# Two sample blocks through one pass of the output and query projections, with the second block's router scores kept and searched later

## The chip, the cores and the metric

The kernel runs on one core of one Trainium2 chip. The metric is the device time of one execution in microseconds (us). All arithmetic is float32. The profile was taken in one execution of its own. That execution has no separate total beside its span, so spans are compared with spans, and the distance from span to timed median is taken as it stands.

## The reference, cut to what matters

A two-layer network works on one block of 128 prompt tokens and on 256 sample tokens, which are two blocks of 128. Per layer and stream:

```
h = layer_norm(x) * (1 + sc1) + sh1
mix = concat(diff_attention, mla, gqa)(h @ w_in) @ w_out        # 20 score maps; a sample block reads 384 keys, the prompt 128
x = layer_norm(alpha * x + g1 * mix, ln1_g, ln1_b)
h = layer_norm(x) * (1 + sc2) + sh2
q = h @ peer_wq ; s = q . keys                                   # 8 retrieval heads, 2 x 128 scores each
top-16 of each half, top-16 of their 256 sums -> 128 experts and gates per token
act = gelu(h . u[expert]) ; ff = sum(gate * act * v[expert])     # u, v: rows of 1024 floats, gathered per token
x = layer_norm(alpha * x + g2 * ff, ln2_g, ln2_b)
```

The experts differ from token to token, so each token block gathers 128 rows of `u` and 128 rows of `v` per token in each layer.

## The kernel before, in words

Five engines each run their own in-order program, made from one list of steps, `STEPS`, written by `plan()`. A step is (kind, layer, stream, block, index). Block 0 is the prompt, blocks 1 and 2 are the sample blocks.

The gathers are the backbone. A step `u` or `v` stands for gathers of 128 rows of 4 KB (0.52 MB each), issued by GpSimd (POOL, L596) into a ring of 15 tiles, `expert`. A `u` tile is consumed by VectorE (DVE, L1434: a dot product for each token), a `v` tile by TensorE (PE, L895: an accumulation into the PSUM tile `acc`, four tiles at a time). Gather number g may be issued only when tile g - 15 has been consumed. Each of the six pairs (layer, block) has 256 gathers: 40 `u` first, then groups of four `v` and four `u`, then the last `v`. I number these six stretches weave 1 to weave 6: prompt, block 1 and block 2 of layer 0, then the same of layer 1.

`weave(l, b, side)` lays other work between the gathers of a pair. Each side step has a planned cost in the table `COST`, and gathers follow in proportion to the cost that has gone by. So the more side work a weave has, the more of it stands between two groups of gathers. The side work of weave k is what weave k + 1 needs, since the indices of a block's experts must be known before its gathers. The side steps that matter here:

- `fin` (DVE, L1466 to L1475): closes the weave before, reads `acc`.
- `ln1`, `h_t`, `win`, `prep`, `k_t`, `cache_t`, `kv_mla`: first norm, transposes, input projection and keys of a stream.
- `q_t`, `q_rope`, `qm_t`, 23 `heads` steps, `mix`: the attention of one block. A full `heads` step has a score matmul (L787), three transposes (L794) and three value matmuls (L814) of three different maps on PE, a maximum on DVE, an exponential and a copy on ScalarE (ACT).
- `wout`: four tiles of the output projection (L706). `ln_x`, `ln_h`: the norms behind it.
- `route`: nine steps, eight with a tile of the query projection (L838) and the matmuls of the scores (L848) one step later.
- `topk` (L1363 to L1382) and `pick` (L1392 to L1421): the search for the 16 best of a retrieval head, and the experts' numbers, all on DVE.
- `idx_t`: transposes the numbers for the `v` gathers. `row`: spreads a row of `mods` over the partitions.

Weights come in tiles of 0.4 to 1.2 MB through a ring of three, `wt`, issued by SyncE (SP, L543) in the order of use. Gathers and weight tiles use the same 16 DMA engines. Before the change `block_steps(l, s, b)` runs attention, `wout`, norms, `route`, `topk` and `pick` for one block, so `w_out` and `peer_wq` with the keys are loaded for each of the three blocks. Scores go to `rs`, two heads deep, and are searched at once.

## Time and profile before

| | us |
|---|---|
| median of 3 timed runs | 2509.18 (2507.83 to 2509.75) |
| span of the profiled execution | 2504.9 |
| outside the span: median less span | 4.3 |
| first gather issued, last gather issued | 215.8, 2475.9 |
| DVE busy, PE busy, POOL busy | 1636.7, 1719.9, 1492.5 |

The page cuts the span into 40 slices of 62.6 us. "DMA" is the mean busy share of the 16 DMA engines. The windows used below run from the first gather of a weave to the first gather of the next, so one window is one weave.

### The profile page before, as it was taken

Reading aid. Unit: us, or ns where it says so; the run is one execution under the profiler, and the core shown is the slowest. Engines: PE = TensorE matmul, PEld = TensorE weight load, DVE = VectorE, ACT = ScalarE, POOL = GpSimd, SP = SyncE. Lnnn points to the kernel's source line nnn. Section 1 sums busy time; section 2 is a strip of 40 time slices with the busy share of each in tenths; the row PEclk is TensorE's granted clock in tenths of the full one; section 3 lists DMA queues with packets and bytes.
Section 4 is the critical chain, followed back from the end, with each engine's and each line's share of the span. In section 5 each row is a group of like instructions: output and inputs, shape, how many; then the busy total and the mean of one; then the engine's idle time right before and its main releaser. Section 6 shows DMA issues by size and latency. Waiting matters only on the chain.

```text
span 2504.9 us, 24629 instructions
## 1 busy us (share of the span) xinstructions
PE 1719.9 (69%) x8433; PEld 838.7 (33%) x8433; DVE 1636.7 (65%) x4033; ACT 334.8 (13%) x990; POOL 1492.5 (60%) x1583
## 2 busy tenths in 40 slices
PE   5888469778287767277877368897738777545557
PEld 3566334442143422132344044355214342101101
DVE  2338886677975782854668857568886568774451
ACT  0410003211131100101111110331112110000000
POOL 1104467656676665666665656665677666777773
PEclk9988789989698878678899678798859889878889
DMA  9768999999999999999999989999999999999996
GB/s 389 305 254 341 412 353 407 411 413 409 410 409 412 406 412 412 374 413 410 410 413 413 378 333 410 411 358 411 411 409 409 412 411 410 409 403 409 410 410 271
DMA packets 248333, 980.67 MB, mean 391 GB/s; under 512 B 28001, under 2 KB 29681, under 8 KB 232849
## 3 DMA queue, kind: packets, MB, share of 16 engines
q0 software_dynamic: 226944, 847.35, 85.1%
q1 hardware_dynamic: 19536, 130.80, 13.0%
q8 instruction: 67, 1.10, 0.2%
q10 hardware_dynamic: 1728, 0.95, 0.1%
q14 instruction: 58, 0.47, 0.0%
HBM read 976.47 MB, written 2.52 MB: 391 GB/s over the span
## 4 chain that ended last, share of the span: by engine, by line
DMA 42%; PE 23%; DVE 19%; POOL 9%; issue 5%; ACT 2%; DVEq 0%; ACTq 0%; POOLq 0%
DMA expert<-in_experts,eidx_t 31%; DVE expert L1434 10%; PE acc L895 10%; POOL expert L596 9%; DMA expert<-in_experts,eidx 8%; PE mmb L696 3%; PE mmb L838 3%; PE mmb L706 2%; DMA expert<-in_w_mod 2%; PE mmb L787 1%; DMA wt<-in_w_wq 1%; ACT hT L975 1%; PE acc L651 1%; PE ob L814 1%; DVE small L1140 1%
## 5 line engine op out<-in xcount | busy, mean ns | idle before, releaser
L1434 DVE CUSTOM_DVE_ANT_0 expert<-expert,hb 128x1024 f32<-128x1024 f32 x768 | 910.0, 1218 | 355.1 <-DMA expert<-in_experts,eidx 335.3
L895 PE MATMUL acc<-expert,strip 128*32 128x512 f32 x3072 | 829.2, 708 | 328.2 <-DMA expert<-in_experts,eidx_t 325.9
L596 POOL DMA_INDIRECT expert<-in_experts,eidx x768 | 734.7, 957 | 491.5 <-PE acc L895 206.8
L596 POOL DMA_INDIRECT expert<-in_experts,eidx_t x768 | 733.2, 955 | 311.4 <-issue 205.7
L895 PEld LDWEIGHTS acc<-expert,strip 128*32 128x32 f32 x3072 | 148.9, 119 | 906.7 <-DMA expert<-in_experts,eidx_t 724.6
L838 PE MATMUL mmb<-hT,wt 128*128 128x128 f32 x1536 | 195.9, 290 | 27.7 <-DMA wt<-in_w_wq 22.8
L838 PEld LDWEIGHTS mmb<-hT,wt 128*128 128x128 f32 x1536 | 189.0, 205 | 51.5 <-issue 45.5
L696 PE MATMUL mmb<-wt,hT 128*128 128x244 f32 x768 | 172.6, 385 | 7.3 <-ACT hT L975 4.8
L696 PEld LDWEIGHTS mmb<-wt,hT 128*128 128x128 f32 x768 | 150.7, 199 | 35.4 <-issue 14.4
L869 PE MATMUL trb<-ident,acts 128*128 128x128 f32 x24 | 9.6, 398 | 194.9 <-DVE acts L1454 194.9
L567 POOL DMA_DIRECT2D expert<-in_w_mod x40 | 21.3, 536 | 181.0 <-PE acc L651 181.0
L1303 DVE TENSOR_REDUCE neg_max<-mmb 128x1 f32<-128x384 f32 (+1 forms) x120 | 54.9, 465 | 101.7 <-PE mmb L787 101.0
L787 PE MATMUL mmb<-area 32*128 32x384 f32 (+5 forms) x240 | 93.0, 494 | 10.1 <-ACT area L1049 5.9
L686 PE MATMUL trb<-ident,tok 128*128 128x128 f32 x144 | 29.3, 338 | 102.1 <-DVEq L1259 61.4
L706 PE MATMUL mmb<-wt,hT 128*128 128x256 f32 x384 | 92.0, 397 | 3.9 <-ACT hT L982 2.7
L912 ACT ACTIVATE area<-mmb 128x256 f32<-128x256 f32 (+3 forms) x126 | 48.5, 387 | 327.8 <-PE mmb L838 290.1
L706 PEld LDWEIGHTS mmb<-wt,hT 128*128 128x128 f32 x384 | 74.5, 198 | 28.2 <-issue 10.0
L1049 ACT ACTIVATE area<-mmb,neg_max 128x384 f32<-128x384 f32 (+1 forms) x120 | 60.8, 507 | 108.9 <-DVE neg_max L1303 108.5
L869 PEld LDWEIGHTS trb<-ident,acts 128*128 128x128 f32 x24 | 3.9, 163 | 207.9 <-DVE acts L1454 201.9
L676 PE MATMUL mmb<-mods,sel 128*128 128x512 f32 x144 | 70.7, 618 | 0.3 <-ACT rows L912 0.3
L1363 DVE MAX8 area<-area 128x8 f32<-128x128 f32 x96 | 23.3, 284 | 69.9 <-ACT area L912 69.3
L1099 ACT ACTIVATE gelu<-gelu 128x32 f32<-128x32 f32 x24 | 5.5, 229 | 472.4 <-DVE gelu L1446 472.4
(177 smaller groups left out, 1615.8 us busy)
## 6 DMA issues: line engine op xcount, KB each, us to landing
wt<-in_w_wq SPq DMA_DIRECT2D x48, 1152.0 KB, 8.4
expert<-in_w_mod POOLq DMA_DIRECT2D x40, 1024.0 KB, 9.3
wt<-in_w_win SPq DMA_DIRECT2D x32, 976.0 KB, 8.1
wt<-in_w_wout SPq DMA_DIRECT2D x24, 1024.0 KB, 8.1
expert<-in_experts,eidx POOLq DMA_INDIRECT x768, 14.0
expert<-in_experts,eidx_t POOLq DMA_INDIRECT x768, 14.0
wt<-in_w_mod SPq DMA_DIRECT2D x8, 1024.0 KB, 8.4
wt<-in_w_uq SPq DMA_DIRECT2D x6, 384.0 KB, 7.0
```

What stands on the lines that cost most here:

```text
L596: pool.indirect_dma_start(expert[:, g % RING, :], None, table, bass.IndirectOffsetOnAxis(at, 0)).then_inc(landed[g % RING], 16)
L676: pe.matmul(mm_bank(mm + half)[:], sel[:, e:e + 1].to_broadcast([P, P]), mods[:, half * 512:half * 512 + 512], start=True, stop=True).then ...
L686: m = pe.transpose(bank[:, q * P:(q + 1) * P], src[:, c * P:(c + 1) * P], ident[:])
L696: m = pe.matmul(bank[:, jj * 256:jj * 256 + IN_C], hT[:, kt, B[jj] * P:(B[jj] + 1) * P], w[:, kt * IN_C:(kt + 1) * IN_C], start=kt == 0, s ...
L706: m = pe.matmul(bank[:, 0:256], hT[:, kt, b * P:(b + 1) * P], w[:, kt * 256:(kt + 1) * 256], start=kt == 0, stop=kt == KT - 1)
L787: pe.matmul(bank[:, 0:K], q_, k_, start=True, stop=True).then_inc(sc_full, 1)
L838: m = pe.matmul(bank[:, i * P:(i + 1) * P], w[:, kt * 256 + i * P:kt * 256 + (i + 1) * P], hT[:, kt, b * P:(b + 1) * P], start=kt == 0, st ...
L895: m = pe.matmul(acc[32 * i:32 * i + 32, cs], strip[:, q % 2, i, at:at + 32], expert[:, (g + i) % RING, cs], start=k < 4, stop=False, skip_ ...
L912: act.activation(dst, src_of(mmb[u % 2]), ACT.Copy).then_inc(mm_free, 1)
L1049: act.activation(E[:, m % 2, 0:K], mmb[at_mm[m] % 2][:, 0:K], ACT.Exp, bias=neg_max[:, m:m + 1], accum_out=row_sum[:, m:m + 1]).then_inc(m ...
L1303: v.tensor_reduce(neg_max[:, m:m + 1], mmb[at_mm[m] % 2][:, 0:K], X, ALU.max, negate=True).then_inc(nmax_ready, 1)
L1434: v.tensor_tensor_reduce(expert[:, r, :], expert[:, r, :], hb[:], 1.0, 0.0, ALU.mult, ALU.add, dots[:, k:k + 1]).then_inc(dot_ready, 1)
```

## The change

Both sample blocks' attention is done first. Then one pass over the four `wout` tiles and the eight `wq` tiles serves both: `wout` multiplies each tile with both blocks one after the other, `route` streams 256 token columns past each weight. Block 1's scores go to `rs` and are searched at once, as before. Block 2's go to `kept`, which lies where the keys were, and are searched in the next weave by `search_steps`. Block 2's activations live in `tok2`, in `wide`. The prompt's layer-1 work up to its attention moves from weave 3 to weave 2, and a wait on `idx_ready` keeps its keys from overwriting `kept`. The gain rows `row` are spread once for both blocks.

```diff
+JOINT = {"wout": 7.2, "route": 2.4}
 def cost_of(x):
-    c = COST[x[0]]
+    c = JOINT.get(x[0], COST[x[0]]) if x[2] == "S" else COST[x[0]]
...
+def block_steps(l, s):
+    b = BLOCKS[s][0]
+    out = [x for c in BLOCKS[s] for x in head_steps(l, s, c)]
     out += [("wout", l, s, b, n) for n in range(OUT_T)]
-    out += [("ln_x", l, s, b, i) for i in range(3)] + [("ln_h", l, s, b, 0), ("h_t", l, s, b, 2)]
+    out += [("ln_x", l, s, c, i) for i in range(3) for c in BLOCKS[s]]
+    for c in BLOCKS[s]:
+        out += [("ln_h", l, s, c, 0), ("h_t", l, s, c, 2)]
...
+def search_steps(l):
+    half = R_HEADS // 2
+    return [x for e in range(2) for x in
+            [("topk", l, "S", 2, half * e + i) for i in range(half)]
+            + [("pick", l, "S", 2, 2 * e + i) for i in range(2)] + [("idx_t", l, "S", 2, e)]]
...
-    steps += weave(0, 0, search + [x for x in sample if x[0] != "win"] + key_steps(0, "S") + block_steps(0, "S", 1), project)
-    steps += weave(0, 1, fins(0, 0) + block_steps(0, "S", 2) + mod_steps(1, (4, 5)) + [("cols", 1, "", 0, 1)])
-    steps += weave(0, 2, fins(0, 1) + ln1_steps(1, "P", 0) + win_steps(1, "P") + key_steps(1, "P") + block_steps(1, "P", 0))
+    again = ln1_steps(1, "P", 0) + win_steps(1, "P") + key_steps(1, "P") + block_steps(1, "P")
+    mix = again.index(("mix", 1, "P", 0, 0))
+    steps += weave(0, 0, search + [x for x in sample if x[0] != "win"] + key_steps(0, "S") + block_steps(0, "S"), project)
+    steps += weave(0, 1, fins(0, 0) + search_steps(0) + mod_steps(1, (4, 5)) + [("cols", 1, "", 0, 1)] + again[:mix])
+    steps += weave(0, 2, fins(0, 1) + again[mix:])
     steps += weave(1, 0, fins(0, 2) + ln1_steps(1, "S", 1) + ln1_steps(1, "S", 2) + win_steps(1, "S") + key_steps(1, "S")
-                   + block_steps(1, "S", 1))
-    steps += weave(1, 1, fins(1, 0) + block_steps(1, "S", 2))
+                   + block_steps(1, "S"))
+    steps += weave(1, 1, fins(1, 0) + search_steps(1))
...
-                    for kt in range(KT):
-                        m = pe.matmul(bank[:, 0:256], hT[:, kt, b * P:(b + 1) * P], w[:, kt * 256:(kt + 1) * 256],
-                                      start=kt == 0, stop=kt == KT - 1)
+                    for jj in range(NB):
+                        for kt in range(KT):
+                            m = pe.matmul(bank[:, jj * 256:jj * 256 + 256], hT[:, kt, B[jj] * P:(B[jj] + 1) * P],
+                                          w[:, kt * 256:(kt + 1) * 256], start=kt == 0, stop=kt == KT - 1)
...
-                                m = pe.matmul(bank[:, i * P:(i + 1) * P], w[:, kt * 256 + i * P:kt * 256 + (i + 1) * P],
-                                              hT[:, kt, b * P:(b + 1) * P], start=kt == 0, stop=kt == KT - 1)
+                                m = pe.matmul(bank[:, i * NB * P:(i + 1) * NB * P],
+                                              w[:, kt * 256 + i * P:kt * 256 + (i + 1) * P],
+                                              hT[:, kt, b * P:(b + NB) * P], start=kt == 0, stop=kt == KT - 1)
...
                 if kind == "k_t":
+                    if s == "P" and l > 0:
+                        act.wait_ge(idx_ready, 2 * 3 * l)
...
+                        if s == "S":
+                            act.wait_ge(mm_full, n("mm_full", 0) + 1)
+                            act.activation(kept[:, e - 1], mmb[at_s % 2][:, 256:512].rearrange("p (i c) -> p i c", i=2),
+                                           ACT.Copy)
...
-                    halves = [(i, 2 * e + i, rs[:, e % 2, i, :]) for i in range(2)]
+                    halves = [(i, 2 * e + i, kept[:, e, i, :] if b == 2 else rs[:, e % 2, i, :]) for i in range(2)]
```

SyncE's loads from the last `win` tiles of layer 0's sample stream to the `mod` tiles, before:

```order
L543 DMA wt<-in_w_uq 128x768
L543 DMA wt<-in_w_wout 128x2048 x4
L543 DMA wt<-in_w_wq 128x2304 x8
L543 DMA wt<-in_w_uq 128x768
L543 DMA wt<-in_w_wout 128x2048 x3
L551 DMA cache<-in_cache 128x928
L543 DMA wt<-in_w_wout 128x2048
L543 DMA wt<-in_w_wq 128x2304 x8
L543 DMA wt<-in_w_mod 128x2048 x8
```

and of the change:

```order
L572 DMA wt<-in_w_uq 128x768 x2
L572 DMA wt<-in_w_wout 128x2048 x3
L580 DMA cache<-in_cache 128x928
L572 DMA wt<-in_w_wout 128x2048
L572 DMA wt<-in_w_wq 128x2304 x8
L572 DMA wt<-in_w_mod 128x2048 x8
```

One set of four `wout` and eight `wq` tiles is gone from each layer.

VectorE in the first `u` tiles of weave 2, from the end of `fin` on, before (L1434 is one `u` tile; 12 of them follow in a row, then the rope of block 2's attention):

```order
L1475 TENSOR_TENSOR x<-tmp,rows 128x1024
L1434 ISA expert,dots<-expert,hb 128x1024
L1434 ISA dots 128x1
L1434 ISA expert,dots<-expert,hb 128x1024
L1434 ISA dots 128x1
```

and of the change, where four `u` tiles (the last is the first row here) are followed by a whole `topk` (L1408 to L1428), and then by eight more `u` tiles and the next `topk`:

```order
L1480 ISA expert,dots<-expert,hb 128x1024
L1480 ISA dots 128x1
L1408 MAX area<-area 128x8 x2
L1411 MAX_INDEX i<-area 128x8
L1412 MATCH_REPLACE area<-area 128x128
L1411 MAX_INDEX i<-area 128x8
L1412 MATCH_REPLACE area<-area 128x128
L1417 MAX area<-area 128x8 x2
L1420 MAX_INDEX i<-area 128x8 x2
L1422 TENSOR_TENSOR area<-area 128x256
L1424 MAX area<-area 128x8
L1425 MAX_INDEX bi<-area 128x8
```

The search that stood behind block 2's own projections at the end of weave 2 now stands at its start, eight `topk` and two pairs of `pick` within the first 64 `u`.

TensorE between two groups of four `v` tiles (L895) in the attention of weave 4, before, four `heads` steps:

```order
L895 MATMUL acc<-expert,strip 32x512 x8
L787 MATMUL mmb<-area 128x384
L794 MATMUL trb<-ident,area 128x128 x3
L814 MATMUL ob<-wide,area 128x64 x2
L814 MATMUL ob<-cache,area 128x64
L787 MATMUL mmb<-area 128x384
L794 MATMUL trb<-ident,area 128x128 x3
L814 MATMUL ob<-area 128x64 x3
```

and of the change, the same stretch from its second step on (six steps stand between the two L927):

```order
L817 MATMUL mmb<-area 128x384
L824 MATMUL trb<-ident,area 128x128 x3
L844 MATMUL ob<-area 128x64 x3
L817 MATMUL mmb<-area 128x384
L824 MATMUL trb<-ident,area 128x128 x3
L844 MATMUL ob<-area 128x64 x3
L817 MATMUL mmb<-area 128x384
L824 MATMUL trb<-ident,area 128x128 x3
L844 MATMUL ob<-wide,area 128x64 x2
L844 MATMUL ob<-cache,area 128x64
L927 MATMUL acc<-expert,strip 32x512 x8
```

Where four or five `heads` steps stood between two groups of `v`, there are now six in weave 4 and five or six in weave 1.

## Rows read from the trace of the kernel before

**Rows 1.** The page, busy share of the DMA engines in 40 slices

```profile
DMA  9768999999999999999999989999999999999996
```

**Rows 2.** Windows, one a weave: us, busy time (count) by engine, PEclk, DMA share, GB/s

```profile
215.80:604.80 389.00, 283.60 (x1475) 168.07 (x1475) 296.68 (x777) 60.01 (x177) 244.51 (x256) 0.87 1.00 398
604.80:980.30 375.50, 262.51 (x1234) 113.17 (x1235) 265.95 (x639) 50.69 (x142) 245.58 (x257) 0.83 1.02 410
980.30:1379.80 399.50, 274.43 (x1258) 129.05 (x1252) 255.51 (x645) 48.79 (x161) 243.55 (x256) 0.82 1.01 406
1379.80:1781.80 402.00, 291.40 (x1460) 164.23 (x1459) 285.18 (x707) 67.50 (x189) 247.00 (x256) 0.82 0.97 385
1781.80:2146.60 364.80, 250.91 (x1158) 112.52 (x1158) 268.50 (x645) 49.24 (x137) 245.72 (x257) 0.84 1.03 410
2146.60:2475.90 329.30, 177.60 (x531) 33.69 (x532) 170.58 (x306) 10.09 (x33) 240.50 (x255) 0.81 1.02 408
```

**Rows 3.** Line L596, the gathers: who waited for them, and issue to landing

```profile
  DVE expert L1434: 335.3, 106
...
DMA to landing us min/median/max: 4.4/14.0/27.1
```

**Rows 4.** DMA issues of the two projections: count, KB each, us to landing

```profile
wt<-in_w_wq SPq DMA_DIRECT2D x48, 1152.0 KB, 8.4
wt<-in_w_wout SPq DMA_DIRECT2D x24, 1024.0 KB, 8.1
```

**Rows 5.** Timeline of DVE, weave 1: one topk, then u tiles

```profile
229.75 0.48 DVE L1363 MAX8 area<-area 128x8 f32<-128x128 f32 x2
...
235.42 1.22 DVE L1434 CUSTOM_DVE_ANT_0 expert<-expert,hb 128x1024 f32<-128x1024 f32 x1
...
236.57 1.22 DVE L1434 CUSTOM_DVE_ANT_0 expert<-expert,hb 128x1024 f32<-128x1024 f32 x1
```

**Rows 6.** Timeline of DVE: a pair of pick to the next topk; fin's middle piece

```profile
564.41 0.22 DVE L1392 CAST area<-i 128x128 f32<-128x128 uint32 x1
...
575.20 0.49 DVE L1363 MAX8 area<-area 128x8 f32<-128x128 f32 x2
...
630.01 1.22 DVE L1470 SCALAR_TENSOR_TENSOR tmp<-x,tmp 128x1024 f32<-128x1024 f32 x1
...
636.13 1.22 DVE L1434 CUSTOM_DVE_ANT_0 expert<-expert,hb 128x1024 f32<-128x1024 f32 x1
```

**Rows 7.** Windows of lost DMA time, same columns as rows 2

```profile
1040.00:1060.00 20.00, 8.21 (x24) 6.16 (x24) 19.29 (x43) 3.38 (x9) 11.73 (x13) 0.59 0.82 299
1420.00:1476.00 56.00, 15.59 (x66) 11.03 (x67) 45.45 (x99) 7.69 (x22) 25.29 (x27) 0.56 0.79 295
1640.00:1664.00 24.00, 20.65 (x115) 12.00 (x114) 16.34 (x37) 7.68 (x24) 11.65 (x13) 0.79 0.76 283
226.00:292.00 66.00, 26.95 (x138) 24.35 (x138) 60.49 (x170) 4.04 (x12) 39.12 (x42) 0.74 1.02 411
```

**Rows 8.** Timeline of PE, weave 4: heads steps at full and half clock

```profile
1631.18 0.91 PE L787 MATMUL mmb<-area 64*128 64x384 f32 x2
...
1633.11 0.91 PE L787 MATMUL mmb<-area 64*128 64x384 f32 x2
...
1606.62 1.64 PE L787 MATMUL mmb<-area 32*128 32x384 f32 x2 [0.52 <-ACT area L1049]
...
1610.20 1.64 PE L787 MATMUL mmb<-area 32*128 32x384 f32 x2
```

**Rows 9.** Timeline of PE, weave 4: route with scores and v; wout

```profile
1769.20 3.84 PE L838 MATMUL mmb<-hT,wt 128*128 128x128 f32 x32
1772.87 0.61 PE L848 MATMUL mmb<-wt,area 128*128 128x128 f32 x4
1773.41 1.92 PE L895 MATMUL acc<-expert,strip 128*32 128x512 f32 x16
...
1674.74 3.72 PE L706 MATMUL mmb<-wt,hT 128*128 128x256 f32 x16
```

More of the change, by code:

```diff
@@ L255, in rows_wanted @@
     kind, l, s, b, e = x
+    if kind == "ln_x" and b == 2:
+        return ()
     st = {"P": 0, "S": 1}.get(s, int(b > 0))
@@ L267, in after, with last_use @@
             return i - 2 if e == 0 else steps.index((kind, l, s, b, 0))
-        return steps.index({0: ("wout", l, s, b, OUT_T - 2), 2: ("ln_x", l, s, b, 0)}[e])
+        return steps.index({0: ("wout", l, s, b, OUT_T - 2), 2: ("ln_x", l, s, BLOCKS[s][-1], 0)}[e])
+    def last_use(i, x):
+        kind, l, s, b, e = x
+        return steps.index((kind, l, s, BLOCKS[s][-1], e)) if kind == "ln_x" else i
     put, released = {}, []
@@ L442, in trunk_program @@
                                                   (512,))
-        qT, rs, rep, cand, cand2, eq, v16, i16f, best, bf, e1 = views(
-            KV, AREA, (2, 2, P), (2, 2, P), (2, P), (16, 16), (256,), (4, TOPK, 16), (16, TOPK), (R_HEADS, 2, TOPK),
+        kept, qT = views(0, KV, (R_HEADS, 2, P), (2, 2, 2 * P))
+        rs, rep, cand, cand2, eq, v16, i16f, best, bf, e1 = views(
+            KV, AREA, (2, 2, P), (2, P), (16, 16), (256,), (4, TOPK, 16), (16, TOPK), (R_HEADS, 2, TOPK),
             (R_HEADS, TOPK), (SLOTS,), (SLOTS,))
@@ L548, in _ @@
                     if n > 0:
-                        end = max(i for i, y in enumerate(STEPS) if y[0] == "wout" and y[1] == n - 1 and y[3] == 2 and y[4] == 0)
+                        end = max(i for i, y in enumerate(STEPS) if y[0] == "wout" and y[1] == n - 1 and y[2] == "S" and y[4] == 0)
                         sp.wait_ge(mm_free, mm_after[end])
@@ L680, in _ @@
                     pe.wait_ge(tok_ready, n("tok"))
-                    src = tok[:]
+                    src = tok2 if (b, e) == (2, 2) else tok[:]
                     for half in range(2):
@@ L846, in scored @@
                         pe.wait_ge(mm_free, use + 1)
-                        for i in range(2):
-                            m = pe.matmul(bank[:, i * P:(i + 1) * P], qT[:, (e - 1) % 2, i, :],
+                        for jj, i in itertools.product(range(NB), range(2)):
+                            m = pe.matmul(bank[:, (2 * jj + i) * P:(2 * jj + i + 1) * P],
+                                          qT[:, (e - 1) % 2, i, jj * P:(jj + 1) * P],
                                           w[:, 2048 + i * P:2048 + (i + 1) * P], start=True, stop=True)
@@ L1344, in _ @@
                     if e == 2:
[L1345 to L1347 removed]
+                        link(v.tensor_tensor(y, y, row() if b < 2 else row_now[-2], ALU.mult))
+                        link(v.tensor_tensor(x[:, b, :], y, row() if b < 2 else row_now[-1], ALU.add))
+                        if b != 1:
+                            v.sem_inc(rows_used, 2)
                 if kind == "ln_h":
[L1350 removed]
+                    normed(tok2 if b == 2 else tok[:], x[:, b, :])
                     v.sem_inc(tok_ready, 1)
```

36 lines of the change are left out of this document (20 added, 16 removed).

## The prediction

> **What bounds the kernel now.** I read the page first. From the fifth slice to the last but one the DMA engines are busy at 9 tenths or more, with one slice at 8 [rows 1], so the transfers are the suspect and not an engine. The second view is one window for each weave [rows 2]. Weave 6 has no weight tile at all and takes 329.3 us for 256 gathers, 1.286 us each, at 408 GB/s. Weave 5 differs in its transfers only by one `uq`, four `wout` and eight `wq` tiles. By the sizes in [rows 4] these are 4 x 1.05 + 8 x 1.18 MB and 0.39 MB, 14.0 MB together, or 34 us at 410 GB/s. It takes 35.5 us longer. So a byte of weights costs its full time there. The third view is the line of the gathers: VectorE waits 335 us for them, and a gather lands 14.0 us after its issue where the least is 4.4 us [rows 3]. The difference, 9.6 us, is queueing. I take it as the cover of the ring: an engine may be 9.6 us late with its tiles before the DMA engines run dry. The fourth view is the stretches in which they did run dry [rows 7]. Against the full share of 1.02, they lose 4 us of 20 at 1040, 13 us of 56 at 1420 and 6 us of 24 at 1640. In the first two VectorE is the busy one (19.3 of 20 us at 1040), in the third TensorE (20.7 of 24). Time that the DMA engines lose is not made up, since POOL needs 240 to 247 us of its own for 256 gathers plus its issue gaps, and the transfers leave no room.
>
> **Weights no longer loaded.** SyncE's order shows four `wout` and eight `wq` tiles fewer in each layer: 8 x 1024 KB + 16 x 1152 KB = 27.3 MB. At 410 GB/s this is 66.5 us less transfer. Weaves 3 and 5 lose these loads, and part of the prompt's loads move from weave 3 to weave 2. This is the gain, if the DMA engines stay fed.
>
> **The kept search at the start of weave 2.** Before, `topk` stood beside `route` steps, whose tiles kept the DMA engines in work. Now eight `topk` and four `pick` stand with no load beside them, among the first 64 `u`. VectorE's work from `fin` to the last `pick`: 60 `u` at 1.15 us (start to start, [rows 5]) is 69.0; eight `topk` at 5.67 (229.75 to 235.42, [rows 5]) is 45.4; two pairs of `pick` at 10.8 (564.41 to 575.20, [rows 6]) is 21.6; `fin` is 6.1 (630.01 to 636.13) and three operations at 1.22 for the rest [rows 6], 9.8. Sum 145.8 us. In the same stretch 60 `u` and 28 `v` are gathered, 88 x 1.286 = 113.2 us. VectorE falls 32.6 us behind, the ring covers 9.6, and 23 us of transfer time are lost. Bounds: if the ring covers all 14.0 us of [rows 3] and the prefetched `mod` tiles fall into the gap (three of 1 MB, 7.7 us), 11 us; if nothing is covered, 33. The window from 226 to 292 speaks for the low end, for there VectorE was busy for 60.5 of 66 us and the DMA engines stayed at 1.02 [rows 7]; but `win` tiles stood beside that search. Weave 5's search, spread over a weave with nothing else in it, brings VectorE 2.9 us for each group of eight gathers beside 4.6 of `u`, against 10.3 of transfer: free.
>
> **TensorE in weaves 1 and 4.** Matmul work is moved, not saved. Prices: a full `heads` step 1.9 us at the 2.4 GHz level (granted clock 1.00; 1631.18 to 1633.11, [rows 8]); four `v` 1.9; a route tile 3.7 us for 32 passes of 128 columns; scores 0.54; a `wout` tile 3.7 us for 16 passes of 256 columns [rows 9]. A pass thus costs 0.115 us at 128 columns and 0.23 at 256: double. So I price a joint route step at 32 x 0.23 + 1.1 = 8.5 us and a joint `wout` at 7.4, each twice the old.
>
> In weave 4, the ten groups of eight gathers with attention and `wout` hold 40 full `heads` steps' worth, 76 us; transposes and latent queries of both blocks, some 8 (my estimate, from 16 transposes and the `uq` matmuls at the prices above); ten times four `v`, 19; `wout` 30; a gain row 2: 135 us. Transfers there: 103 + 4 x 2.56 + 1 = 114. Excess 21, less the cover: 11 us. In its routes, 36 gathers and eight tiles take 46.3 + 8 x 2.88 = 69 us, TensorE 68 + 8 x 1.9 + 4 = 87: excess 18, less the cover: 8 us, of which part was already lost before in the third stretch of [rows 7]. Before, 6 us were lost here, and I count 13 more. In weave 1, attention is spread thinner: 13 groups, 140 us of TensorE against 145 of transfer, nothing lost; its routes have 86 to 88 against 80, within the cover. At 1.2 GHz a `heads` step takes 3.6 us (1606.62 to 1610.20, [rows 8]). TensorE idles before the attention begins, as before, so I allow one more group of four to six steps at that level, 7 us. Term: +20. Bounds: 0 if the excess hides in a full cover of 14 us twice and the pieces overlap; 45 with no cover and two such groups.
>
> The rule that speaks against the doubled price is in the Trainium skill, "TensorE: Matmul & The Clock Gate", section "Back-to-back issue gap": sustained spacing grows only from about 81 ns at 128 columns to about 131 ns at 512, the weight load being part of both. By it a joint route tile would cost less than twice one tile, and this term would be some 8 us smaller for weave 4's routes. The rows here are float32 with 0.115 against 0.23 us, and the sum goes by them.
>
> **What becomes lighter.** Weave 3 no longer has `ln1` in its first `u` tiles; the 4 us lost at 1040 go: -4. The three gain rows saved per layer, the extra ACT copies of 256 columns (ACT is busy for 60 to 68 of 390 to 402 us in weaves 1 and 4, [rows 2]) and the wait of the prompt's keys on `idx_ready` cost nothing: behind that wait on ACT stand the copies for the prompt's `k_t`, which come 60 `u` after the last `pick`. If that cover were gone, ACT would hold TensorE's `kv_mla` for the length of a `pick`, 6 us.
>
> **Sum.** -66.5 + 23 + 20 - 4 = -27.5. The span goes from 2504.9 to 2477.4; with the 4.3 us between span and median, 2482.
>
> **Rivals.**
> 1. *The ring covers nearly all* (chance 0.18). +11 and +5 in place of +23 and +20: 2455 to 2462. For it: weave 1 had TensorE and VectorE both near full at places and a DMA share of 1.00 [rows 2]. Against it: weave 4 lost time with less work in it.
> 2. *TensorE sets the pace of weaves 1 and 4, and the kernel is slower* (0.14). Place: the 80 full `heads` steps, six to a group in weave 4. At 1.9 us six steps and four `v` need 13.3 us where a group of gathers needs 10.3, so all hangs on their price. The maxima are on VectorE behind `u` tiles that wait for gathers, and when TensorE idles it falls to the level at which a step costs 3.6. If half the steps run at 3.6, that is 40 x 1.7 = 68 us more, less some slack in weave 1: about 2535. It decides from 2.2 us a step on (80 x 0.34 = 27 us eats the gain). For it: the 24 us at 1640 with 0.79 of the clock [rows 7]. Against it: dense stretches keep TensorE busy, and busy stretches had the full clock.
> 3. *The losses just eat the gain* (0.08): terms at +33 and +30: within 0.2% of before, 2504 to 2514.
> 4. *Weight bytes are worth little because transfers hide elsewhere*: weaves 5 and 6 in [rows 2] exclude it. That the loads are not removed is excluded by SyncE's order.
>
> **How the numbers follow.** My forecast, 2470 to 2500, has 0.52; rival 1 has 0.18; a gain of 5 to 9 us between it and rival 3 has 0.08; rival 3 has 0.08 and rival 2 has 0.14. A measurement of this kernel can tell about 0.2%, 5 us, from no change. So: faster 0.78, same 0.08, slower 0.14. The range leaves out the worst of rival 2 and the best of rival 1: 2461 to 2512.
>
> **What would show it.** The DMA page should have some 27 MB less on the hardware queue. Weave 5's window should be near 330 us and weave 3's near 362 (329 and 13.6 MB). Weave 2 should have a stretch of about 130 us after its start in which VectorE is busy above 0.9 and the DMA share is near 0.85. Weaves 1 and 4 should be longer than before only by a few to 25 us. The prediction is wrong if weave 4 grows by more than 45 us (rival 2), if the search does not thin the transfers (rival 1), or if a tile of the joint route takes much less than 7 us.

## The result: slower, and where the time went

The changed kernel takes 2629.2 us (median of 4 runs, 2621.4 to 2635.2) against 2508.5 (2502.7 to 2509.8) of the kernel before on the same chip: a ratio of 1.047, 95% interval 1.045 to 1.050. I had forecast 2482. The profiled span went from 2504.9 to 2619.6, +114.7.

The page of the changed kernel: busy tenths of the DMA engines in 40 slices of 65.5 us, GB/s in the same slices (the answer to [rows 1]) and the hardware queue: packets, MB, share.

```profile
DMA  9878898897979999999999999879699999999997
GB/s 381 308 272 344 318 347 336 315 374 279 390 286 339 413 413 410 409 411 410 411 410 411 373 380 390 304 250 356 240 337 375 409 409 409 409 409 409 409 410 290
q1 hardware_dynamic: 16080, 103.54, 10.1%
```

The queue moves 103.54 MB, 27.3 less than before (130.80 there). The bytes are gone as forecast, but slices that read 9 now read 6 to 8 in two places, between the fifth and the twelfth and between the 26th and the 29th. The windows of the six weaves, from first gather to first gather as in [rows 2], say which weaves these are:

```profile
215.80:684.60 468.80, 361.48 (x1827) 240.68 (x1831) 317.18 (x821) 92.67 (x263) 243.86 (x256) 0.83 0.89 336
684.60:1085.70 401.10, 226.47 (x944) 78.36 (x937) 268.67 (x678) 33.43 (x126) 245.15 (x257) 0.75 0.97 378
1085.70:1446.80 361.10, 223.58 (x933) 83.70 (x928) 243.50 (x579) 27.12 (x79) 243.90 (x256) 0.80 1.03 411
1446.80:1928.70 481.90, 367.97 (x1807) 231.31 (x1811) 302.44 (x752) 98.93 (x274) 246.36 (x256) 0.84 0.87 326
```

Weaves 5 and 6 take 332.7 and 329.2 us. Against [rows 2] the six weaves changed by +80, +26, -38, +80, -32 and 0. By rate times length the bytes left weaves 3 and 5 (14 and 18 MB less); weaves 1 and 4 move 2 to 3 MB more than before.

I keep a ledger. In a window, the transfer time lost is its length times (1 - its GB/s / 410), 410 GB/s being what the full stretches of both traces show (weave 3 here, 411; weave 5 before, 410). Weave 4 lost 482 x (1 - 326/410) = 99 us, where it had lost 24 before.

| transfer time lost, us | weave 1 | 2 | 3 | 4 | 5 | 6 | sum |
|---|---|---|---|---|---|---|---|
| before | 12 | 0 | 4 | 24 | 0 | 1 | 42 |
| changed | 84 | 31 | 0 | 99 | 11 | 0 | 225 |

(The sums are of unrounded values.)

+183 us lost and -66.5 us of bytes is +117, the +115 of the span. Of the four terms, the bytes and weave 3 came as priced and the kept search cost 31 + 11 where I had 23. The term "TensorE in weaves 1 and 4" was +20 and measured +147.

Weave 4, cut at the ends of its kinds of TensorE work, shows where. The rows are: to the last `win`; to `kv_mla`; both attentions; the joint `wout`; the norms to the last `h_t`; the joint routes.

```profile
1446.80:1592.20 145.40, 96.59 (x417) 61.52 (x419) 108.51 (x235) 15.38 (x38) 85.66 (x90) 0.81 0.96 372
1592.20:1621.90 29.70, 15.09 (x64) 5.39 (x64) 16.15 (x37) 7.82 (x29) 20.59 (x21) 0.71 1.03 411
1621.90:1759.90 138.00, 119.30 (x627) 69.74 (x625) 74.97 (x165) 50.85 (x142) 65.56 (x70) 0.84 0.81 287
1759.90:1798.20 38.30, 36.82 (x176) 26.81 (x180) 12.20 (x22) 4.36 (x10) 17.28 (x19) 0.96 0.97 368
1798.20:1846.30 48.10, 20.15 (x89) 6.07 (x88) 44.30 (x101) 7.45 (x18) 29.19 (x28) 0.74 0.88 315
1846.30:1928.50 82.20, 79.82 (x448) 61.69 (x451) 46.12 (x191) 12.89 (x36) 28.08 (x29) 0.97 0.73 266
```

By the last column the six stretches lost 13, 0, 41, 4, 11 and 29 us. The same stretches of the kernel before, where the third holds one attention (the first two, 183.8 and 26.6 us, lost 17 and 0):

```profile
1590.20:1661.30 71.10, 63.74 (x337) 35.33 (x341) 43.29 (x95) 25.50 (x71) 41.50 (x45) 0.81 0.94 370
1661.30:1683.80 22.50, 21.13 (x113) 14.36 (x116) 11.13 (x20) 3.54 (x7) 17.01 (x19) 1.00 1.01 392
1683.80:1708.10 24.30, 14.44 (x50) 4.33 (x52) 22.24 (x51) 4.27 (x9) 15.23 (x16) 0.78 1.02 411
1708.10:1776.20 68.10, 58.29 (x430) 40.63 (x433) 54.38 (x203) 8.89 (x27) 37.82 (x40) 0.93 1.02 412
```

The attention went from 71.1 us with 45 gathers to 138.0 with 70. Who holds up POOL in weave 4 of the changed kernel, by the waits of its engine:

```profile
POOL expert L625 <- PE acc L927: 114.0, 25, 24.6
POOL expert L625 <- DVE dots L1480: 66.1, 50, 5.3
```

It waits 114 us for a ring tile that TensorE has not yet consumed (53.3 before) and 66 us for one of VectorE's. A piece of TensorE's timeline in the second attention shows how one such wait arises:

```profile
1740.02 0.91 PE L817 MATMUL mmb<-area 64*128 64x384 f32 x2
1741.64 0.39 PE L844 MATMUL ob<-cache,area 128*128 128x64 f32 x2
1745.55 0.33 PE L901 MATMUL trb<-ident,acts 128*128 128x128 f32 x1 [3.53 <-DVE acts L1500]
1745.81 1.65 PE L817 MATMUL mmb<-area 64*128 64x384 f32 x2
1749.39 3.52 PE L927 MATMUL acc<-expert,strip 128*32 128x512 f32 x16
```

TensorE stands for 3.5 us at the transpose of `acts`, which VectorE makes behind its `u`. The next score matmul then takes 1.65 us in place of 0.91 and the four `v` 3.52 in place of 1.9: the lower clock level. POOL waits 6.8 us for the end of those `v`. All of TensorE's idle time in the attention is 19 us of 138; in the rest it works.

In one session of the experiments (runs e7, e9, e10 and e11) the kernel before itself took 2654 us, so e7, e9 and e10 are read by their ratio to it alone and e11, which has none, is not read.

### The profile page after: what moved, and what is told of

Read it like the earlier page. It is cut to its first block, busy times and chain, and to the rows that moved or that the text cites. A ratio compares the mean times of both kernels' runs of the same rounds, so it can differ in the third digit from the quotient of the medians.

```text
span 2619.6 us, 23419 instructions
## 1 busy us (share of the span) xinstructions
PE 1724.2 (66%) x7897; PEld 825.3 (32%) x7897; DVE 1639.2 (63%) x4033; ACT 321.5 (12%) x962; POOL 1488.4 (57%) x1583
## 3 DMA queue, kind: packets, MB, share of 16 engines
q1 hardware_dynamic: 16080, 103.54, 10.1%
## 4 chain that ended last, share of the span: by engine, by line
PE 31%; DMA 30%; DVE 25%; POOL 8%; issue 5%; ACT 2%; DVEq 0%; ACTq 0%; POOLq 0%
DMA expert<-in_experts,eidx_t 21%; DVE expert L1480 11%; PE acc L927 9%; POOL expert L625 8%; DMA expert<-in_experts,eidx 6%; PE mmb L868 5%; PE mmb L725 3%; PE mmb L736 3%; PE mmb L817 2%; PE ob L844 2%; DMA expert<-in_w_mod 1%; PE trb L824 1%; DVE small L1182 1%; PE acc L680 1%; PE trb L715 1%
## 5 line engine op out<-in xcount | busy, mean ns | idle before, releaser
L927 PE MATMUL acc<-expert,strip 128*32 128x512 f32 x3072 | 829.6, 748 | 354.5 <-DMA expert<-in_experts,eidx_t 350.8
L927 PEld LDWEIGHTS acc<-expert,strip 128*32 128x32 f32 x3072 | 151.8, 125 | 946.6 <-DMA expert<-in_experts,eidx_t 728.2
L868 PE MATMUL mmb<-hT,wt 128*128 128x128 f32 (+1 forms) x1024 | 186.3, 344 | 10.2 <-DMA wt<-in_w_wq 5.4
L868 PEld LDWEIGHTS mmb<-hT,wt 128*128 128x128 f32 x1024 | 165.1, 204 | 36.9 <-issue 17.1
L596 POOL DMA_DIRECT2D expert<-in_w_mod x40 | 21.3, 537 | 181.1 <-PE acc L680 181.1
L944 ACT ACTIVATE area<-mmb 128x256 f32<-128x256 f32 (+4 forms) x94 | 39.7, 425 | 271.3 <-PE mmb L868 249.4
L1083 ACT ACTIVATE area<-mmb,neg_max 128x384 f32<-128x384 f32 (+1 forms) x120 | 60.7, 506 | 55.5 <-DVE neg_max L1346 55.0
L1075 ACT ACTIVATE area<-trb 128x384 f32<-128x384 f32 (+1 forms) x120 | 50.1, 417 | 123.0 <-PE trb L824 122.4
L705 PE MATMUL mmb<-mods,sel 128*128 128x512 f32 x120 | 63.6, 664 | 0.0
```

The lines of the kernel that those rows point to most:

```text
L705: pe.matmul(mm_bank(mm + half)[:], sel[:, e:e + 1].to_broadcast([P, P]), mods[:, half * 512:half * 512 + 512], start=True, stop=True).then ...
L868: m = pe.matmul(bank[:, i * NB * P:(i + 1) * NB * P], w[:, kt * 256 + i * P:kt * 256 + (i + 1) * P], hT[:, kt, b * P:(b + NB) * P], start= ...
L927: m = pe.matmul(acc[32 * i:32 * i + 32, cs], strip[:, q % 2, i, at:at + 32], expert[:, (g + i) % RING, cs], start=k < 4, stop=False, skip_ ...
L1083: act.activation(E[:, m % 2, 0:K], mmb[at_mm[m] % 2][:, 0:K], ACT.Exp, bias=neg_max[:, m:m + 1], accum_out=row_sum[:, m:m + 1]).then_inc(m ...
```

## The experiments

### Would it fit if the gathers stood elsewhere? (e1, e2, e8)

```diff
-JOINT = {"wout": 7.2, "route": 2.4}
+JOINT = {"wout": 7.2, "route": 8.0}                   # e1
+JOINT = {"wout": 7.2, "route": 8.0, "heads": 3.2}     # e2
```

> The changed kernel, with the planned cost of a joint route step raised from 2.4 to 8.0, so that more gathers stand among the joint routes and fewer among the attention steps of weaves 1 and 4; no work is added or left out. Theory A (spacing: the side work of weaves 1 and 4 would fit under the transfers, but the planner's costs put too much TensorE work between two groups of v, and the ring runs dry): the routes' stretches lose 15 to 25 us less each and attention a little more; about 2600 to 2615. Theory B (weaves 1 and 4 hold a serial chain through TensorE, VectorE and ACT that is itself longer than the transfers, wherever the gathers stand in it): within 10 us of 2629, the loss only changes place.

> As the run before, and the planned cost of a heads step also raised from 2 to 3.2, so that in weaves 1 and 4 the gathers follow TensorE's time more closely and fewer of them stand among the norms, inputs and keys. Theory A (spacing): weaves 1 and 4 lose together some 80 of their 183 us; about 2550 to 2580. Theory B (serial chain): 2615 to 2640.

Measured: e1 2589.7 us (ratio 1.034, 1.031 to 1.037) and e2 2581.2 (1.031, 1.027 to 1.035). e1 gave back 40 us, more than theory A had asked for. e2 gave only 9 more and stands just above theory A's range, far below theory B's. Weaves 1 and 4 of e2:

```profile
216.60:656.70 440.10, 351.90 (x1827) 236.73 (x1831) 316.79 (x821) 93.21 (x263) 246.14 (x256) 0.86 0.92 354
1420.20:1884.20 464.00, 363.90 (x1807) 231.34 (x1811) 301.70 (x752) 99.57 (x274) 244.85 (x256) 0.85 0.90 337
```

With the places tuned, weaves 1 and 4 of e2 are 440 and 464 us, still 51 and 62 longer than before. So the places of the gathers are part of the loss, 29 + 18 us in these two weaves, and by these two settings of the costs not the larger part; no other setting was tried. One caution goes with every single window here: weave 1 of e14 below has the same steps as weave 1 of e2 and took 428.2 us in place of 440.1, with TensorE busy for 343.7 in place of 351.9 us at a granted clock of 0.88 in place of 0.86.

The same edit in the kernel before:

```diff
-        "ln_h": 5.2, "route": 1.5, ...
+        "ln_h": 5.2, "route": 4.2, ...
```

> The kernel before with one number changed: the planned cost of a route step from 1.5 to 4.2, which is what it takes on TensorE; only the places of the gathers among the side steps move. The ledger of before has 12, 4 and 24 us of transfer time lost in weaves 1, 3 and 4. Theory A (a good part of these losses is routes packed too close): 2485 to 2500. Theory B (the weaves are bound by their whole sum of work and the places matter little): 2503 to 2512.

Measured: 2528.1 us, ratio 1.008 (1.005 to 1.011): slower by 0.8%, outside both expectations. Weave 1 lost 22 us in place of 12 and weave 4 kept its 24. Matching a planned cost to TensorE's time is no gain by itself. Weave 1 grew by 10 us, and TensorE was busy there for 295.5 us in place of 283.6 at a granted clock of 0.81 in place of 0.87 [rows 2], so the lower clock can account for what weave 1 lost; why it was lower is open.

### The second attention left out (e3)

```diff
-    out = [x for c in BLOCKS[s] for x in head_steps(l, s, c)]
+    out = [x for c in BLOCKS[s] for x in head_steps(l, s, c) if c < 2 or x[0] in ("mix", "h_t")]
...
-        ends = [i for i, x in at if x[0] == "heads" and x[1] == l - 1 and x[3] == 2]
+        ends = [i for i, x in at if x[0] == "heads" and x[1] == l - 1 and x[3] == 1]
```

> The changed kernel without the attention of sample block 2 in both layers (its queries, rope and 23 heads steps are left out; its mix still copies what lies there), so weaves 1 and 4 keep the joint output projection, the joint routes and all gathers. Theory C (the second attention is the cost that I priced too low): weaves 1 and 4 lose at most 15 us each of transfer time, each window falls by 65 to 75 us, about 2485 to 2500. Theory D (the joint routes and norms behind are the cost): the loss in the routes' stretches stays, 35 to 45 us in each of the two weaves; about 2540 to 2570.

Measured: 2513.1 us, ratio 1.002 (0.999 to 1.004), between the two. Weaves 1 and 4:

```profile
227.60:643.60 416.00, 316.92 (x1593) 206.24 (x1593) 305.55 (x796) 69.49 (x199) 245.98 (x257) 0.86 0.96 375
1400.20:1839.70 439.50, 337.64 (x1571) 207.17 (x1575) 286.17 (x705) 75.45 (x209) 244.57 (x257) 0.82 0.93 357
```

Weave 1 fell by 53 us and weave 4 by 42. The other 27 and 37 us by which they exceed the kernel before belong to the joint `wout`, norms and routes. Neither half of the work alone is the cause: both were priced too low. The division is rough. The profiled execution was the slowest of nine, 2532.6 us against their median of 2513.1; 12 of these 20 us lie ahead of weave 1 (first gather at 227.6 in place of 215.8), and up to 8 may lie in the weaves, so the attention's share may be larger than these windows say.

### How long is the computing alone? (the light runs)

```diff
-            table = t_in["experts"].rearrange("e (h d) -> (e h) d", h=2)
+            table = t_in["experts"].rearrange("e (h d) -> (e h) d", d=256)
...
-                    pool.indirect_dma_start(expert[:, g % RING, :], None, table, bass...
+                    pool.indirect_dma_start(expert[:, g % RING, 0:256], None, table, bass...
...
-                        v.tensor_tensor_reduce(expert[:, r, :], expert[:, r, :], hb[:], 1.0, 0.0,
+                        v.tensor_tensor_reduce(expert[:, r, :], expert[:, r, :], hb[:], 0.1, 0.0,
```

A gather brings 1 KB a row in place of 4. Every step stays; the sums are of other data.

> The changed kernel with gathers of 256 in place of 1024 floats per row (the rest of a ring tile keeps old values, so dot products and sums are of other data); every instruction of VectorE, TensorE, ACT and POOL stays, only the gathered bytes fall to a quarter. Weaves 2, 3, 5 and 6 then go at the pace of POOL or VectorE, about 300 to 320 us each. Theory B (weaves 1 and 4 are a chain of computing that is longer than the transfers): they still take 430 us or more each. Theory A or any in which they only lose by the meeting of late tiles and transfers: they fall below 380 us each.

> The kernel before, with gathers of 256 in place of 1024 floats per row as in the light run of the changed kernel (dot products and sums are of other data, all instructions stay). It shows the pace of the computing alone, weave by weave. Theory B (in weaves 1 and 4 the computing alone already took nearly as long as the transfers, so that whatever was added there fell on the end): weave 1 takes 355 to 385 us and weave 4 380 to 400 us, and the changed kernel's light run is longer in each by 70 to 90. Rival (there were some 40 us of room in each, as I had reckoned for TensorE in the prediction, and another thing ate the time): weaves 1 and 4 below 350 us.

Spans: 2497.3 us for the changed kernel and 2303.1 for the kernel before. Weaves 1, 4 and 6 of the light run of before:

```profile
218.30:587.40 369.10, 275.80 (x1511) 173.10 (x1511) 293.63 (x777) 60.24 (x177) 246.38 (x256) 0.81 0.49 159
1251.00:1636.10 385.10, 267.58 (x1460) 162.29 (x1457) 288.32 (x725) 67.62 (x189) 247.37 (x257) 0.81 0.45 144
1965.80:2285.10 319.30, 181.31 (x533) 34.33 (x532) 166.45 (x296) 9.83 (x32) 241.62 (x256) 0.79 0.37 107
```

The attention and the routes of its weave 4:

```profile
1446.50:1517.40 70.90, 63.50 (x338) 35.31 (x339) 43.32 (x95) 25.51 (x71) 44.40 (x48) 0.81 0.38 117
1564.10:1625.70 61.60, 54.02 (x432) 40.10 (x435) 51.61 (x190) 8.99 (x27) 34.33 (x35) 0.89 0.54 180
```

Weaves 1 and 4 of the light run of the changed kernel, then weave 4's attention and routes:

```profile
218.60:671.30 452.70, 346.99 (x1827) 234.67 (x1831) 316.86 (x821) 92.89 (x263) 247.63 (x256) 0.85 0.41 129
1358.00:1828.50 470.50, 357.10 (x1774) 231.05 (x1777) 302.28 (x752) 99.19 (x274) 249.17 (x256) 0.83 0.36 114
```

```profile
1521.90:1660.30 138.40, 120.78 (x627) 69.98 (x625) 74.93 (x165) 51.04 (x142) 66.16 (x70) 0.83 0.29 88
1745.10:1828.30 83.20, 80.83 (x448) 62.40 (x451) 46.11 (x191) 12.91 (x36) 28.15 (x29) 0.96 0.35 117
```

This is the decisive pair. With the DMA engines busy for four tenths of the time, weaves 1 and 4 of the changed kernel take 453 and 471 us, only 16 and 11 less than in full. The attention takes 138.4 against 138.0 and the routes 83.2 against 82.2. So these weaves are a chain of computing, and the transfers wait for it. In the kernel before the chain was 369 and 385 us already, with transfers worth 378 (155 MB at 410 GB/s): there was little room to put anything in. The chain grew by 84 and 85 us, the windows by 80 and 80. The attention of weave 4 before was paced by computing too: 70.9 us light against 71.1 in full. Its routes were not, 61.6 against 68.1.

Two limits of this pair. Each light run is one execution, and that of the kernel before had weave 1 at a granted clock of 0.81 where the full run had 0.87, so its 369 us are rather too many for the full run. And the chain is that of one order of steps: e2, with other places for the gathers, takes 440 and 464 us in full, less than the 453 and 471 here.

### Which engine makes the chain? (e11, e12, e5, e13)

```diff
-                        v.tensor_tensor_reduce(expert[:, r, :], expert[:, r, :], hb[:], 0.1, 0.0,
+                        v.tensor_tensor_reduce(expert[:, r, 0:256], expert[:, r, 0:256], hb[:, 0:256], 0.1, 0.0,
```

> The changed kernel's light run with the dot products of u also over 256 in place of 1024 floats (VectorE's instructions stay, each takes a third or less; about 100 us less of VectorE in each weave). It asks which engine makes the chain of weaves 1 and 4. If it is TensorE with its own waits: their attention, wout and route stretches (138, 37 and 83 us in weave 4) stay within 5 us, and the weave falls only where norms and first steps stand, by 20 to 45 us to 425 to 450. If it is VectorE's u between the maxima and sums of attention: the attention stretch falls by 20 us or more, weave 4 below 420.

> The light run with short dot products once more. If TensorE with its own waits makes the chain of weaves 1 and 4: their attention, wout and route stretches (138, 37 and 83 us in weave 4) stay within 5 us and the weave falls only where norms and first steps stand, to 425 to 450 us. If VectorE's u are part of it: the attention stretch falls by 20 us or more, weave 4 below 420.

e11 (span 2687.5 us) is not read. e12, the same kernel, has a span of 2382.3; its weave 4, in the six stretches:

```profile
1275.70:1390.80 115.10, 82.27 (x384) 58.87 (x387) 62.46 (x235) 15.49 (x39) 88.16 (x89) 0.85 0.48 151
1390.80:1417.50 26.70, 15.66 (x63) 5.54 (x62) 9.86 (x37) 7.81 (x29) 20.09 (x22) 0.68 0.41 118
1417.50:1559.00 141.50, 131.47 (x627) 77.95 (x625) 48.85 (x165) 50.75 (x142) 66.83 (x71) 0.75 0.29 88
1559.00:1597.40 38.40, 36.90 (x177) 26.93 (x180) 4.37 (x22) 4.36 (x10) 17.56 (x19) 0.96 0.48 158
1597.40:1636.60 39.20, 19.71 (x88) 5.83 (x88) 33.47 (x107) 7.45 (x18) 27.48 (x27) 0.74 0.38 114
1636.60:1719.80 83.20, 80.83 (x448) 62.52 (x451) 44.23 (x184) 12.88 (x36) 30.32 (x31) 0.96 0.36 121
```

With the `u` short, attention, `wout` and routes of weave 4 keep their length (141.5, 38.4 and 83.2 us): TensorE paces them. In the attention this has two parts. TensorE's idle time fell from 18 to 10 us, but its granted clock was 0.75 against 0.83 and its busy time grew by 11. So some of its waits there were VectorE's doing, up to 8 us, and the lower clock took their place in this run. The first steps and keys (164 to 142) and the norms (48 to 39) shrink: VectorE is in the chain there. Weave 4 comes to 444 us, within the first expectation. Weave 1 comes to 400, 53 less than in the light run: its first steps and keys fell by 29 us and its norms by 10, and its attention from 134 to 123, where TensorE's busy time fell by 5 with a higher granted clock (0.90 against 0.87). So VectorE's part in the chain of weave 1 is larger than in that of weave 4. This is one execution.

A known dose of TensorE taken out:

```diff
-                                m = pe.matmul(bank[:, i * NB * P:(i + 1) * NB * P], ..., hT[:, kt, b * P:(b + NB) * P], ...
+                                m = pe.matmul(bank[:, i * NB * P:i * NB * P + P], ..., hT[:, kt, b * P:(b + 1) * P], ...
```

> The changed kernel with 128 token columns behind each weight of the joint routes in place of 256 (block 2's queries are left out; its scores are of old values); all steps, loads and gathers stay. It takes about 4 us of TensorE from each of eight tiles, 32 us in each of weaves 1 and 4. Theory B (all of it lies on the path): 55 to 70 us less than 2629, so 2560 to 2575. Rival (the routes cost only what they exceed their stretch by, as in my sum, 8 us a weave): 2605 to 2620.

Measured: 2592.3 us, between the two. The routes of weave 4:

```profile
1840.30:1895.80 55.50, 53.12 (x448) 42.29 (x451) 40.94 (x168) 12.73 (x36) 27.18 (x29) 0.95 0.90 346
```

82.2 us became 55.5, all of the dose of TensorE (79.8 to 53.1). The window fell by 22 us and weave 1's by 17. In weave 4 the attention was 4 us longer, at a granted clock of 0.81 in place of 0.84. The DMA share in the routes rose from 0.73 to 0.90: near the transfers' own pace less than the whole dose can come back.

A known dose of VectorE taken out:

```diff
-                    if e == 1:
+                    if e == 1 and b < 2:
                         normed(y, y)
...
-                    normed(tok2 if b == 2 else tok[:], x[:, b, :])
+                    if b < 2:
+                        normed(tok[:], x[:, b, :])
```

> The changed kernel without the two normalisations of sample block 2 behind the joint wout (its gains and sums stay): 2 x 4.9 = 9.8 us of VectorE less in each of weaves 1 and 4, where TensorE has only v to do. Theory B (a serial chain, VectorE's norms in it): weaves 1 and 4 fall by 7 to 11 each, 2608 to 2616. If TensorE's total alone sets these weaves: within 6 us of the changed kernel's 2629.

Measured: 2606.8 us, just under theory B's range; the span is 2608.3, which is 11 less than the changed kernel's span, where the medians differ by 22. The norms of weave 4:

```profile
1793.90:1834.90 41.00, 21.53 (x89) 6.19 (x88) 37.71 (x75) 7.45 (x19) 27.86 (x27) 0.75 0.94 349
```

48.1 became 41.0 us. VectorE's busy time fell by 8.5 us in each of the two weaves (302.4 to 293.9 in weave 4). Weave 1 fell by 8 us as expected, weave 4 by only 4, since its attention was 3 us longer, here too at 0.81 in place of 0.84. So a dose of either engine shows nearly whole in its own stretch, and with half of its size or more in the weave (27 us of TensorE: 22 and 17; 8.5 of VectorE: 8 and 4): the stretches stand one behind the other.

### How much room had the kernel before? (e6)

```diff
-                        for i in range(2):
+                        for i in (0, 1, 0, 1):
                             for kt in range(KT):
                                 m = pe.matmul(bank[:, i * P:(i + 1) * P], w[:, kt * 256 + i * P:...
```

> The kernel before with the matmuls of each query tile issued twice (same result): 8 x 3.7 = 30 us more of TensorE in each of the prompt's start and the five weaves that route, with no other change. Theory B (weaves 1 and 4 have almost no room for TensorE, weaves 2, 3 and 5 have much): weaves 1 and 4 grow by 20 to 35 us each, weaves 2, 3 and 5 by less than 10 each, the prompt's routes ahead of weave 1 by 15 to 30; in all 2565 to 2605. Rival (room in every weave, the ring covers it): every weave grows by less than 10, 2525 to 2545.

Measured: 2546.8 us, ratio 1.016 (1.012 to 1.020), between the two. The first gather comes 25 us later, weave 1 is 15 longer, weave 4 only 7, and weaves 2, 3, 5 and 6 by -6, +6, -3 and -5. Theory B was wrong on weave 4: its routes had room, though its attention had none. The routes went from 68.1 to 83.2 us, 15 for some 30 of TensorE added, and the attention before them was 4 us shorter, at a granted clock of 0.90 in place of 0.81. So about half of the dose was hidden, and part of the rest was given back by the clock. At 83.2 us these routes are as long as the joint ones of the changed kernel (82.2), yet 41 gathers stand in them and 8 us of transfer are lost, against 28 gathers and 29 us there: the same TensorE time costs less where more gathers stand beside it. A line of the trace tells attention and routes of the kernel before apart. From issue to landing a gather took, in the attention and then in the routes of weave 4 of the kernel before:

```profile
DMA to landing us min/median/max: 4.4/7.8/11.8
...
DMA to landing us min/median/max: 12.4/18.1/21.1
```

and in the attention of weave 4 of the changed kernel:

```profile
DMA to landing us min/median/max: 4.1/6.0/7.0
```

Where a gather lands after 18 us, half of 30 us of TensorE in a stretch of 68 is hidden. Where it lands after 6 to 8 us, of a least of 4.1 to 4.4, hardly a transfer is queued and there is next to no cover.

### The kept search spread out (e10, e14)

```diff
-fins(0, 0) + search_steps(0) + mod_steps(1, (4, 5)) + [("cols", 1, "", 0, 1)] + again[:mix])
+fins(0, 0) + fill(search_steps(0), mod_steps(1, (4, 5)) + [("cols", 1, "", 0, 1)] + again[:keys],
+                  {"topk": 1.7, "pick": 1.7}) + again[keys:mix])
```

Both with the costs of e2; `keys` is the place of the prompt's `k_t`.

> The changed kernel with the costs of e2, and the kept search of weave 2 laid between the mod tiles, the prompt's first norm and its input projection, in place of ahead of them all. It tests my second term alone: if weave 2's loss of 27 us is VectorE being full for a stretch with no load beside it, weave 2 falls from 403 to 380 to 388 and the whole to about 2558 to 2566. If weave 2 is long by its whole work, it stays at 398 or more, about 2576 to 2585.

> The mixed search once more, against 2581 of e2: weave 2 falls from 403 to 380 to 388 and the whole to 2558 to 2566 if the loss is VectorE being full ahead of all loads; 2576 or more if weave 2 is long by its whole work.

e10 had a ratio of 1.039 (1.031 to 1.046) and decides nothing. e14, the same kernel, took 2559.5 us, ratio 1.021 (1.015 to 1.027), as expected. Weave 2 of e2, then of e14:

```profile
656.70:1059.70 403.00, 226.92 (x948) 80.75 (x940) 268.43 (x678) 33.34 (x126) 244.77 (x257) 0.76 0.97 382
```

```profile
650.00:1034.40 384.40, 224.13 (x945) 76.70 (x938) 268.67 (x678) 33.53 (x126) 243.85 (x257) 0.78 1.01 402
```

The work is the same and 18.6 us are gone. Weave 2 with the search ahead of all loads took 393 to 403 us in six runs (the changed kernel, e1, e2, e3, e5, e13), so 384 is outside their spread. Weave 1, which the edit doesn't touch, was 12 us shorter all the same, so the total's 22 are not all the edit's. My mechanism for the kept search holds. This is the fastest form of the change that I ran, and it is still 2% slower than the kernel before.

### Work moved out of weave 4 (e7, e9, e15)

```diff
-fins(0, 1) + ln1_steps(1, "P", 0) + ...
+fins(0, 1) + ln1_steps(1, "S", 1) + ln1_steps(1, "P", 0) + ...
...
-fins(0, 2) + ln1_steps(1, "S", 1) + ln1_steps(1, "S", 2) + ...
+fins(0, 2) + ln1_steps(1, "S", 2) + ...
```

> The changed kernel with the planned costs of e2 (joint route 8.0, heads 3.2) and layer 1's first norm of block 1 with its transposes moved from the start of weave 4 to the start of weave 3, where nothing waits for it. It takes 4.4 us of VectorE and 1.8 to 3.5 of TensorE out of weave 4's chain. Theory B (the chain of weave 4 is its length): weave 4 falls by 5 to 9 us against 464, about 2572 to 2577. If the places of the gathers decide: no change, 2578 to 2585.

> The kernel before with only that move: layer 1's first norm of block 1 with its transposes stands at the start of weave 3 in place of weave 4. Theory B (weave 4 of before is paced by its own steps, 385 us of them by the light run): 4 to 9 us faster, 2499 to 2505. If before is bound by its transfers in weave 4: within 3 us of it; weave 3, which loses 4 us at its start already, may lose 2 to 4 more.

> The kernel before with the early norm of block 1 once more. By the slow session's ratio of 1.008 it would take 2520 to 2535; by theory B 2499 to 2505; if the place of 5 us in weaves 3 and 4 does not matter, 2505 to 2512.

e7 (in the changed kernel, where the moved norm overwrites the prompt's attention output in `tok`, so that its `mix` copies other data) had a ratio of 1.034 (1.026 to 1.041); it can't be told from e2. e9, the kernel before with the move, had 1.008 (1.004 to 1.012), slower where both of its expectations were faster or level. e15, the same kernel as e9, took 2500.6 against 2504.0, ratio 0.997 (0.995 to 1.000), in theory B's range. Its weave 4:

```profile
1383.80:1772.50 388.70, 289.29 (x1451) 165.86 (x1451) 286.32 (x710) 64.47 (x181) 243.44 (x256) 0.86 1.01 402
```

402.0 became 388.7 us, at a granted clock of 0.86 in place of 0.82. That is more than the 4.4 + 3.5 us moved, and it comes back in part: weave 3 lost 10 us in place of 4. In all it is 3 us, at the edge of what can be told, and e9 had the opposite sign. So it is not shown that the move gains.

## Why the prediction was wrong

**What bounds the kernel: right for four weaves.** "A byte of weights costs its full time" held where I had read it. Weaves 3 and 5 are 361.1 and 332.7 us where I had put 362 and 330. I then took this bound for all six. The light run shows that weaves 1 and 4 of the kernel before had two bounds of almost the same size, transfers of 378 us and a chain of computing of 369 and 385. I took the DMA shares of 1.00 and 0.97 in [rows 2] for proof that only the transfers counted there.

**Weights no longer loaded, -66.5: right** in bytes and in time. The bytes left weaves 3 and 5, which are 38 and 32 us shorter; weaves 1 and 4 never had fewer to move. The term for weave 3, -4, came too.

**The kept search, +23: right in mechanism**, shown by e14. It measured 31 in weave 2, within the bounds, in a stretch of 170 us (690 to 860) in which VectorE was busy for 164. "Spread over a weave with nothing else in it ... free" was wrong for weave 5, which lost 11, 8 of them between 1948.7 and 1988.7, where VectorE was busy for 39 of 40 us.

**TensorE in weaves 1 and 4, +20: the step that failed.** It counted only what TensorE exceeds the transfers by in a stretch, less a cover, as if the rest of the chain hid. What stands in those weaves, +72 and +75 us of lost transfer time, goes with the growth of the whole chain, 84 and 85 us in the light runs. The prices of single operations held: a joint route tile is 6.9 to 7.1 us in the chain of the light run, against my 7.4 without the scores. That is 0.216 to 0.222 us for a pass of 256 columns against 0.115 for one of 128, nearly double, so no cheaper pass is to be had from twice the columns here:

```profile
1775.44 6.91 PE mmb L869 x32
1785.09 7.10 PE mmb L869 x32
```

Three other things in the step failed:

- *The balance was drawn for two stretches and not for the weave.* I compared 135 against 114 us and 87 against 69 and let the rest of weave 4 lose nothing more. The norms, doubled to 48 us with VectorE as their pace, had no row in my sum and lost 11. (The first steps lost 13, but they had lost 17 before.) In weave 1 I compared 140 against 145 and 87 against 80 and forecast no loss at all; attention and `wout` took 179 us there with 162 of TensorE and lost 30, the routes 20.
- *TensorE's busy time was taken for the length of the stretch.* Attention and `wout` of weave 4 hold 119.3 + 36.8 = 156 us of TensorE, where I had 135, and last 176. The 20 between are its waits, the longest 4.6 us for exponentials and 3.5 for `acts`. 45 us were lost there, where my excess was 21.
- *The cover was subtracted twice, and the changed kernel has next to none.* I took 9.6 us off each excess, from the median landing of the whole kernel. In the attention of weave 4 the landing was 7.8 us before, and is 6.0 now, of a least of 4.4 and 4.1. In the routes it was 18.1 before, so there was a cover there; in the changed kernel the norms ahead of them already land at 5.8 and the routes at 6.2. Stretches that stand one behind another in a slow chain find the ring as the last one left it.

In all, weave 4's stretches lost 13, 0, 41, 4, 11 and 29 us where they had lost 17, 0, 7, 1, 0 and 0: the growth is in the attention (34), the routes (29) and the norms (11). I had put 11 in attention and `wout`, 8 in the routes and 7 for the clock, and took 6 off as lost already. Those 6, at 1640 in [rows 7], lie in the attention, and not in the routes as I wrote; the routes of before lost nothing. There is a slip in rival 3 as well: its terms give -7.5 us and so 2502, and not 2504 to 2514.

**Rival 2** named the right weaves and the right sign, with 0.14, and its first half holds: TensorE paces attention, `wout` and routes of weave 4. Its price, heads steps at the lower level and a turning point at 2.2 us a step, is not what made weave 4 long, and its 2535 us is 94 short of the measured time: by the records of the granted clock TensorE was busy at the lower level for 82 us in weave 4, against 77 before, and the mean clock there is 0.84 against 0.82 of [rows 2]. In weave 1 it was 92 us against 49, mean 0.83 against 0.87. The four `v` took 3.52 us at the lower level against 1.9, nearly twice, so up to some 22 us of weave 1's 80 may be the clock's (an estimate: half of the 43 us more at the lower level); no run separates that.

**How far this is shown.** Shown are the chain's growth and the engines that pace the stretches of weave 4. Measured with an uncertainty of some 10 us a weave are its two halves (the second attention 42 to 53 us a weave, the joint remainder 27 to 37) and the share of the gathers' places, 47 us by e2. Argued only is how the waits in the attention come about one by one.

## What to carry to other kernels

Before moving work into a stage whose transfers look full, measure how long its computing is alone: shrink the transfers and leave every instruction. A stage with transfers and a serial chain of equal length has little room in either, whatever the busy shares of its engines say. Read the cover of a ring (issue to landing) in the very stretch that gets the work, and draw the balance over the whole stage, idle time of the chain included.

## What the runs showed of the hardware

Quarter-size gathers hardly speed up a weave that does nothing else. Weave 6 takes 319.3 us for 256 gathers of 1 KB rows against 329.3 with 4 KB, 1.247 against 1.286 us each. In the changed kernel's light run, where weave 6 takes 319.6 us, POOL waits almost only for its own issue, and a gather lands 2.7 us after it:

```profile
POOL expert L626 <- issue: 69.5, 228, 0.3
POOL expert L626 <- PE acc L928: 7.6, 25, 0.3
```

POOL's 242 us of busy time and these 70 make 311 of its 319.6. So the pace of issuing lies only 3% under that of the transfers, and fewer bytes in the gathers would gain little in such a weave. Where weight tiles share the DMA engines it is different: in the light run of the kernel before, weaves 2, 3 and 5 take 326, 337 and 330 us against 375.5, 399.5 and 364.8 in full, and the whole span is 202 us shorter.
